# Where the weight splits stand in the rounds of two engines in the mixture-of-experts stage

## The reference

```python
def moe_ffn(h, router, w_gu, w_down):
    logits = (h @ router).astype(jnp.float32)
    top_val, top_idx = lax.top_k(logits, TOP_K)
    weights = jax.nn.softmax(top_val, axis=-1)
    gate = jnp.sum(jax.nn.one_hot(top_idx, N_EXPERTS, dtype=jnp.float32) * weights[..., None], axis=-2)
    out = jnp.zeros(h.shape, jnp.float32)
    for e in range(N_EXPERTS):
        out = out + gate[..., e:e + 1] * swiglu(h, w_gu[e], w_down[e])
    return out
```

## Time and profile before

| | |
|---|---|
| median of 3 runs | 2097.06 us (2095.42 to 2097.63) |
| the profiled execution | 2097.63 us, its span 2095.8 us |
| instructions | 28640 |
| expert stage in the profile | about 727 to 1718 us after the span's start |
| TensorE matmuls busy | 2003.2 us, 96% |
| VectorE busy | 1720.0 us, 82% |
| ScalarE busy | 1325.6 us, 63% |
| mean granted TensorE clock | 0.98 of full speed |

### The profile page before, as it was taken

How to read it: one execution, slowest core, us unless ns; L and a number is a source line. 1 busy time by engine, 2 the same in 40 slices (tenths; PEclk the granted TensorE clock), 3 DMA queues, 4 the chain that set the end, 5 groups by cost and what they waited for, 6 DMA issues and landing times.

```text
span 2095.8 us, 28640 instructions
## 1 busy us (share of the span) xinstructions
PE 2003.2 (96%) x10424; PEld 1662.4 (79%) x10424; DVE 1720.0 (82%) x2427; ACT 1325.6 (63%) x1972; POOL 0.2 (0%) x4
## 2 busy tenths in 40 slices
PE   6998999998989999999999999999999999999997
PEld 5777899978877788887888888888888866867776
DVE  7688878668776698989989898998989988776664
ACT  4354544355564588878787787878878874444543
POOL 0000000000000000000000000000000000000000
PEclk9999999999999999999999999999999999999999
DMA  9846689846332299989999899999989985663530
GB/s 377 293 148 206 231 313 320 290 147 206 121 111 91 77 374 339 375 319 364 374 337 368 329 375 335 390 348 342 371 325 373 378 320 181 213 210 99 192 111 20
DMA packets 154212, 560.20 MB, mean 267 GB/s; under 512 B 17233, under 2 KB 17489, under 8 KB 153937
## 3 DMA queue, kind: packets, MB, share of 16 engines
q1 hardware_dynamic: 154064, 558.29, 73.3%
HBM read 557.18 MB, written 1.05 MB: 266 GB/s over the span
## 4 chain that ended last, share of the span: by engine, by line
PE 75%; DVE 13%; ACT 6%; DMA 4%; issue 3%; DVEq 0%; SPq 0%; ACTq 0%
PE ps L526 20%; PE ps L528 20%; PE ps L527 20%; PE ps L532 11%; DVE spl L515 5%; PE ps L536 3%; ACT sph L503 2%; DMA ring<-in_moe_gu 2%; DVE macc L579 2%; DVE arena L2163 1%; DMA ring<-in_moe_down 1%; DMA ring<-in_dense_down 1%; ACT arena L2129 0%; ACT arena L770 0%; ACT ps L889 0%
## 5 line engine op out<-in xcount | busy, mean ns | idle before, releaser
L515 DVE TENSOR_TENSOR spl<-ring,sph 128x1024 fp32r<-128x1024 f32 x906 | 1078.7, 1220 | 261.3 <-ACT sph L503 248.5
L503 ACT ACTIVATE sph<-ring 128x1024 fp32r<-128x1024 f32 x906 | 948.9, 1059 | 533.1 <-PE ps L528 369.7
L526 PE MATMUL ps<-sph,hH 128*128 128x512 f32 (+1 forms) x1296 | 520.6, 402 | 1.5 <-DVE hL L883 1.3
L528 PE MATMUL ps<-sph,hL 128*128 128x512 f32 (+1 forms) x1296 | 506.9, 391 | 0.0
L527 PE MATMUL ps<-spl,hH 128*128 128x512 f32 (+1 forms) x1296 | 505.7, 390 | 0.0
L526 PEld LDWEIGHTS ps<-sph,hH 128*128 128x128 f32 x1296 | 245.6, 190 | 52.1 <-issue 3.8
L528 PEld LDWEIGHTS ps<-sph,hL 128*128 128x128 f32 x1296 | 244.6, 189 | 52.4
L527 PEld LDWEIGHTS ps<-spl,hH 128*128 128x128 f32 x1296 | 245.7, 190 | 47.8 <-issue 1.0
L526 PE MATMUL ps<-sph,rH 128*128 128x512 f32 x664 | 271.5, 409 | 5.5 <-ACT arena L3117 2.0
L528 PE MATMUL ps<-sph,rL 128*128 128x512 f32 x664 | 261.4, 394 | 0.0
L527 PE MATMUL ps<-spl,rH 128*128 128x512 f32 x664 | 261.1, 393 | 0.0
(11 more groups left out here) (313 smaller groups left out, 1759.0 us busy)
## 6 DMA issues: line engine op xcount, KB each, us to landing
ring<-in_moe_gu SPq DMA_DIRECT2D x448, 512.0 KB, 5.4
ring<-in_moe_down SPq DMA_DIRECT2D x224, 512.0 KB, 5.3
ring<-in_mod SPq DMA_DIRECT2D x144, 512.0 KB, 4.8
ring<-in_w_in SPq DMA_DIRECT2D x64, 512.0 KB, 4.3
ring<-in_dense_gu SPq DMA_DIRECT2D x44, 512.0 KB, 5.3
ring<-in_ssm_w_in SPq DMA_DIRECT2D x40, 512.0 KB, 3.7
ring<-in_dense_down SPq DMA_DIRECT2D x22, 512.0 KB, 5.5
ring<-in_hyb_w_in SPq DMA_DIRECT2D x20, 512.0 KB, 6.0
```

What stands on the lines that cost most here:

```text
L503: a.activation(k.high[m % SPLITS][:, 0:w], raw[:, 0:w], ACT.Copy).then_inc(k.S.half_rounded, 1)
L515: v.tensor_tensor(k.low[m % SPLITS][:, 0:w], raw[:, 0:w], k.high[m % SPLITS][:, 0:w], ALU.subtract).then_inc(*k.tick(k.S.half_split, f"hal ...
L526: pe.matmul(out, a[0], b[0], start=start, stop=False, skip_group_check=True)
L528: return pe.matmul(out, a[1], b[0], start=False, stop=stop, skip_group_check=True)
```

## The change

In `moe_scalar` and `moe_vector`, for both kinds of pieces, the split is written ahead of `advance` where it stood behind it:

```diff
@@ moe_scalar
             for part in range(4):
+                split_scalar(a, k, k.stream.at["moe_gu", q] + part + SPLITS)
                 advance(live)
-                split_scalar(a, k, k.stream.at["moe_gu", q] + part + SPLITS)
             live.append(gated_scalar(a, k, q))
@@
+                split_scalar(a, k, k.stream.at["moe_down", (q - 3) // 2] + kk + SPLITS)
                 advance(live)
-                split_scalar(a, k, k.stream.at["moe_down", (q - 3) // 2] + kk + SPLITS)
@@ moe_vector
             for part in range(4):
+                split_vector(v, k, k.stream.at["moe_gu", q] + part + SPLITS)
                 advance(live)
-                split_vector(v, k, k.stream.at["moe_gu", q] + part + SPLITS)
             live.append(gated_vector_of(v, k, q))
@@
+                split_vector(v, k, k.stream.at["moe_down", (q - 3) // 2] + kk + SPLITS)
                 advance(live)
-                split_vector(v, k, k.stream.at["moe_down", (q - 3) // 2] + kk + SPLITS)
```

## The result

The kernel before takes 2097.31 us (median of 6 runs, 2094.25 to 2100.75), the changed one 2108.86 us (6 runs, 2104.77 to 2114.84). The ratio is 1.0058, with an interval of 1.0042 to 1.0075: slower by more than 0.2%. The forecast was 2113 us, the range 2102 to 2121. The profiled executions took 2097.63 and 2110.27 us.

The account below looks back on a forecast made before the run. TensorE's pace was taken to bound the expert stage. Fourteen late flips gave +15.7 us, all other terms 0: 2097.63 becomes 2113.3, less 0.6 us for the median, so 2113 us; range 2102 to 2121 us.

Parts of the forecast that it names:

- What bounds the stage: Expert stage: runs at TensorE's pace, busy 978.49 of 982 us; its only tight edge is the flip's wait for VectorE's multiplication.
- The splits forward, worth 0: Splits in the expert stage: pieces ready up to 0.67 us earlier, priced at 0, with 3.5 us gain as far end.
- The delay: Multiplication ahead of the flip: 1.14 us later where VectorE is late, 1.36 us where ScalarE is, never both added.
- 14 tight items at 1.01 to 1.23 us, 15.7 us: Flips behind gathering (7) and collection (7): delay less 0.13 us room, 14.1 to 17.2 us, middle 15.7 us.
- the first rival: Half is paid back: helpers and transfers catch up while TensorE waits; +8 us, 2105 us; chance 0.16.
- Items 12, 26, ... at 0: Items one round after a gathering: the wait before gives their lag back; 0 taken, 9.5 us kept for the range.
- The third rival: More places pay: items one round after a gathering lose time too; 26.7 us in all, 2124 us; chance 0.10.
- the rival of the transfers: Expert stage bound by its transfers, waits made good: 2097 us, down to 2091; chance 0.16 (0.11 same, 0.05 faster).
- Collection, gathering and low part at 0: Collection and gathering one piece later: 0; low part 0.33 us after the multiplication, covered by 0.4 us of transposes.
- The clock: TensorE's clock in the expert stage: stays fully granted through waits of 1 to 1.4 us; nothing charged.
- The marks: Signs of being right: flip waits 14 to 20 us, 14 to 20 times; undisturbed silu 2.3 us after rounding; other stages unchanged.

Follow-up runs that it names:

- e1: Kernel before, with one split put ahead of the small operations only where the items behind a gathering or collection are multiplied: 2108.94 us, ratio 1.0057.
- e3: Kernel before, with split and small operations exchanged only in the two loops over the w_down pieces: 2094.05 us, ratio 0.9999.
- e2: Kernel before, with the exchange made everywhere except the places that serve the items behind a gathering or collection: 2100.34 us, ratio 1.0025.
- e9: Kernel before, with one split put ahead of the small operations only for the seven items behind a gathering: 2100.29 us, ratio 1.0022.
- e11: Kernel before, with two pieces instead of one put ahead of the small operations for the seven items behind a gathering: 2122.07 us, ratio 1.0136.
- e10: Kernel before, with one split put ahead of the small operations only for the seven items behind the collection (and item 2): 2106.03 us, ratio 1.0042.
- e4: Kernel before, with silu and multiplication issued one piece earlier, the flipped block's low part left where it was: 2095.70 us, ratio 1.0003.
- e7: Changed kernel, with silu and multiplication issued ahead of the fourth part's split, the flipped block's rounding and low part staying late: 2112.84 us, ratio 1.0094.
- e5: Kernel before, with the exchange made on ScalarE alone, VectorE keeping its old order: 2108.67 us, ratio 1.0074.
- e8: Kernel before, with the whole small group (silu, rounding, multiplication, low part) issued one piece earlier: 2090.76 us, ratio 0.9984.
- e6: Kernel before, with the exchange made on VectorE alone, except in the step that holds the collection: 2113.30 us, ratio 1.0093.

## Why the prediction was right, and what in it was off

**What bounds the stage: right.** TensorE's pace, and one edge of it. The stage grew by its stands (12.0 of 12.7 us), and e1 gives the loss with 14 places.

**The splits forward, worth 0: right.** e3 is 0.9999, and the stage of e2 has 1.3 us more, not less. Nothing was won from earlier splits.

**The delay: the right size, the wrong path.** I had the 1.14 us of VectorE for items with a backlog and 1.36 us through ScalarE otherwise. Behind a gathering TensorE stands 1.25 us, which with the room of 0.14 us is a delay of 1.39, close to the release's distance of 1.36, although VectorE works through five splits without a pause. The delay enters ahead of the backlog, at the gathering itself. For undisturbed items 1.6 us came out where I had 1.32, since the release that the added piece waits for comes 1.61 us after the one before (775.22 to 776.83), across a flip, and not 1.36. It cost nothing against 2.65 us of room.

**14 tight items at 1.01 to 1.23 us, 15.7 us: the term that was mis-sized.** The seven behind a gathering cost 8.8 us, beside 7.1 to 8.6 forecast. The seven behind the collection cost 3.9 us where the prediction had the same 7.1 to 8.6. The step that failed is the sentence against the first rival, that today's lag is already gone by then since undisturbed items lie between. It isn't: ScalarE waits for landings on the whole way from item 26 to the collection, e9 lets the stands behind the collection go from 3.1 to 0.5 us, e11 to 0, and e10 shows 8.5 us when the gathering isn't touched. Put right, the term is 8.8 + 3.9 = 12.7 us; less the 0.7 us of the next paragraph it is 12.0, and 2097.3 + 12.0 is 2109.3 us, beside 2108.86 measured. The outcome so lies between the forecast and the rival by which half is paid back, just below the forecast's own range of 2109 to 2118. That rival's reason, that part of the lag is that of transfers, is what the traces show.

**Items 12, 26, ... at 0, because the lag is given back: right, and for the reason given.** They lost 0.7 us of stands. The third rival had them pay: in e2, where the gathering's round isn't held, they do, by 2.8 us in all. The odd thing is that the prediction used this argument one round after a gathering and denied it three rounds after.

**Smaller slips of the working.** The delay through ScalarE is worked out as 1.32 us and used as 1.36. The rooms behind a gathering are given as 0.10 to 0.13 us, while its own row for item 24 has 0.15; the trace has 0.12 to 0.15. The forecast's own range of 2109 to 2118 isn't worked out: 14.1 to 17.2 us would make 2111 to 2114. And the range of 2102 to 2121 leaves out all of the rival of the transfers. None of these changes the outcome.

**Collection, gathering and low part at 0: right in the sum, weaker than it was put.** The low part "stays covered" only as long as it follows a late multiplication. e4 and e7 take that away, and TensorE waits 3.3 and 15.1 us for it. The gathering isn't without effect either: its own delay is the way by which the loss comes in.

**The clock: nothing charged for these waits, right.** The stage is granted 1.00.

**The transfers as the bound: excluded for the stage as a whole.** The stage's rate fell to 352 GB/s while TensorE's stands grew, and the slices of after still reach 400 (40 equal slices of the stage, GB/s):

```profile
GB/s 348 376 344 314 377 353 375 330 307 400 332 380 336 303 397 341 366 349 297 391 346 375 350 287 393 342 370 363 282 376 354 369 355 282 385 353 374 355 384 351
```

The rule of the Trainium skill (DMA: Bandwidth & Descriptors, section Bandwidth) that the HBM side binds at about 358 GB/s would have made the stands free; slices of 400 and 405 GB/s lie above that figure. And the stands were not free: 12.0 us of added stands made the stage 12.7 us longer. What the transfers do hold is the helpers, in the rounds behind a gathering.

**The marks.** The wait at the flip is 13.1 us in the rows and 16.1 us as stands, beside the 14 to 20 given, in 14 and 15 places, and the single stands are 0.33 to 1.39 us, beside 0.8 to 1.4; the silu comes after 2.58 us instead of 2.3; the other stages are unchanged, PE being busy 668.00 us of the first 727 beside 667.93 before.

What stays open: why the medians of e2 are 4.0 us apart with 1.3 us in the stage, why either engine alone costs as much as both or more, and the part of e11's median that its profiled execution doesn't show, of which the last section has the clocks.

## What to carry to other kernels

Where an engine works through a long row of prefetch operations and now and then does a short one that the bottleneck waits for, one place in the row decides: take the distance between the short operation's end and its consumer's start, at each kind of place, less the 0.15 us of the hand-over, and compare this room with the delay that the new order brings. That delay is not only the length of one prefetch operation (1.14 us here): if that operation waits for the bottleneck to free a buffer, it is the distance between two such releases (1.36 us, and 1.6 across a flip). Don't add up such places as if each had its own lag. If a wait of the bottleneck comes ahead of another, transfers and helpers catch up during the first, and a wait that is there today may be a debt that the new one pays (3.1 us went to 0.5 in e9). And when one operation of a hand-over is moved earlier, move the whole group: the next one stood at the same 14 places (e7).

## What the runs showed of the hardware

TensorE's granted clock is full over the expert stage in the kernels whose stands in it are up to 1.8 us long (before, after, e1 to e5, e7, e9), and also in e8, with its one wait of 1.9 us at 1708.2. In three kernels it falls, each time for 3.4 us: once in e6 after the stand of 2.24 us, twice in e10, twice in e11. The windows view of e11 behind the stand that ends at 1326.84 us and is 2.90 us long (us, busy time and count of PE, PEld, DVE, ACT, POOL, granted clock, DMA share, GB/s):

```profile
1328.00:1331.40 3.40, 3.40 (x11) 2.65 (x10) 3.19 (x5) 1.26 (x2) 0.00 (x0) 0.56 1.03 416
```

And of e10, behind its stand of 1.90 us that ends at 996.13 (both windows take in some time at the full clock):

```profile
997.20:1000.60 3.40, 3.40 (x11) 2.68 (x10) 3.19 (x5) 2.05 (x4) 0.00 (x0) 0.59 0.94 339
```

In such a fall TensorE is granted the lower of its two levels, 1.2 GHz, and its matmuls start 0.43 us apart where it is 0.23 at full clock (e11, within the fall):

```profile
1328.72 0.63 PE L526 MATMUL ps<-sph,rH 128*128 128x512 f32 x1
1329.15 0.63 PE L527 MATMUL ps<-spl,rH 128*128 128x512 f32 x1
```

Eight of them are 0.20 us late each: about 1.6 us lost per fall. In four of the five cases the fall begins 0.4 to 1.6 us after TensorE has begun to work again. The second of e11 begins while TensorE still stands, 0.4 us before the flip at 1455.06:

```profile
1452.00:1454.70 2.70, 0.32 (x2) 0.00 (x0) 2.27 (x3) 2.38 (x4) 0.00 (x0) 1.00 0.96 360
1454.70:1455.10 0.40, 0.04 (x1) 0.08 (x2) 0.40 (x2) 0.28 (x1) 0.00 (x0) 0.50 1.03 389
```

For e10 this nearly closes the account: stands of 12.1 - 4.1 = 8.0 us and two falls at 1.6 make 11.2 of the stage's 11.7 us. For e6 it gives 16.5 of 17.3 us, and for e11 (with 0.4 us at item 108) 18.3 where the stage is 16.7 longer, so the account is good to about 2 us. Not every long stand is followed by a fall: of the thirteen of 1.9 us and more in e6, e8, e10 and e11 five are, so a stand of 2 us can cost more than it lasts.

e11 fits in: its profiled execution had a mean clock of 0.981 over the kernel, the other four 0.974 to 0.978, and they took 2116.63 to 2125.76 us beside 2109.22. Lower clocks go with longer times there; that the missing part is more such falls in the stage isn't shown, since only one execution has a trace.
